# A three-layer kernel with mixtures of experts: weights placed and loaded earlier, stores moved to another queue, wide products added

## The reference, cut to what matters

```
group_idx   = top 1 of softmax(t @ router_group_w + b)          # 4 groups
exp_idx     = top 2 inside that group                           # 4 experts in each
combine     = one_hot(expert) * gate                            # [512, 16]
h = silu(t @ w_gate[e]) * (t @ w_up[e])                         # 1024 -> 256, every expert e
y = sum over e of combine[:, e] * (h @ w_down[e])               # 256 -> 1024
```

## Time and profile before

| what | value |
|---|---|
| median of 3 runs | 2019.25 us |
| profiled execution, its own time | 2021.44 us |
| its span, first to last instruction | 2019.6 us |
| PE busy | 1928.9 us (96%) |
| DVE, ACT, POOL busy | 950.5, 436.0, 326.3 us |
| mean granted TensorE clock | 0.976 |
| DMA moved | 363.86 MB, mean 180 GB/s |
| passes of the three layers, about | 849 to 1001, 1390 to 1543, 1850 to 1996 us |

### The profile page before, as it was taken

One profiled execution on the slowest core, in us unless ns is written; L12 is line 12 of the kernel. 1 busy time (PEld: TensorE's weight loads), 2 busy tenths in 40 slices (PEclk: granted clock), 3 DMA queues, 4 the chain that ended last, 5 costly groups with the idle time before them and its releaser, 6 DMA issues. The chain is left out here.

```text
span 2019.6 us, 20721 instructions
## 1 busy us (share of the span) xinstructions
PE 1928.9 (96%) x7464; PEld 1024.5 (51%) x7464; DVE 950.5 (47%) x1803; ACT 436.0 (22%) x1051; POOL 326.3 (16%) x548
## 2 busy tenths in 40 slices
PE   8999999999999999999899998999989999999995
PEld 4444444558885444544345445545434656645431
DVE  3444734547775022623363555535343367625333
ACT  1111101013333100100241105511002546612000
POOL 1000000000012000133100006502332003301333
PEclk9999999999999999999888999998998999999998
DMA  6223373730004113699834882027997102027996
GB/s 202 92 104 110 130 260 122 253 126 1 1 1 146 64 61 137 244 369 411 324 132 146 281 323 85 24 104 290 407 405 276 66 24 84 2 85 280 358 413 263
DMA packets 123017, 363.86 MB, mean 180 GB/s; under 512 B 26188, under 2 KB 31592, under 8 KB 110368
## 3 DMA queue, kind: packets, MB, share of 16 engines
q1 hardware_dynamic: 83104, 196.16, 27.2%
q10 hardware_dynamic: 25776, 133.70, 16.6%
q0 software_dynamic: 14032, 32.64, 4.5%
HBM read 335.07 MB, written 39.88 MB: 186 GB/s over the span
## 5 line engine op out<-in xcount | busy, mean ns | idle before, releaser
L1701 PE MATMUL bank<-ring,work 128*128 128x512 f32 (+1 forms) x432 | 201.5, 621 | 13.9 <-issue 13.1
L448 PE MATMUL bank<-featT,ring 128*128 128x512 f32 x384 | 168.7, 593 | 3.0 <-DMA ring<-in_w_in 3.0
L2562 PE MATMUL bank<-ring,featT 128*128 128x512 f32 x384 | 169.9, 603 | 1.6 <-DVE small L2654 1.6
L1409 PE MATMUL bank<-ring,work 128*128 128x512 f32 x384 | 166.5, 593 | 3.0 <-PEq L1200 1.1
L2059 POOL DMA_INDIRECT work<-x_rows,small x132 | 132.1, 1001 | 221.2 <-DVE work L2023 155.1
L1701 PE MATMUL bank<-work 128*128 128x512 f32 (+1 forms) x336 | 152.3, 607 | 0.0
L1701 PEld LDWEIGHTS bank<-ring,work 128*128 128x128 f32 (+1 forms) x432 | 75.9, 181 | 118.9 <-issue 118.8
L1725 DVE TENSOR_TENSOR work<-work,bank 128x256 f32<-128x256 f32 x39 | 16.4, 421 | 229.1 <-ACT work L1722 229.1
L2562 PEld LDWEIGHTS bank<-ring,featT 128*128 128x128 f32 x384 | 73.9, 194 | 93.9 <-issue 92.1
L1409 PEld LDWEIGHTS bank<-ring,work 128*128 128x128 f32 x384 | 72.2, 190 | 91.2 <-issue 91.2
L448 PEld LDWEIGHTS bank<-featT,ring 128*128 128x128 f32 x384 | 71.2, 190 | 83.9 <-issue 80.8
(11 more groups left out here) (503 smaller groups left out, 3045.9 us busy)
## 6 DMA issues: line engine op xcount, KB each, us to landing
ring<-in_w_in SPq DMA_DIRECT2D x15, 2048.0 KB, 11.7
ring_halves<-in_w_ada SPq DMA_DIRECT2D x48, 512.0 KB, 7.1
y_rows<-work ACTq DMA_DIRECT2D x39, 512.0 KB, 12.9
ring<-in_moe_w_gate ACTq DMA_DIRECT2D x14, 1024.0 KB, 9.2
ring<-in_moe_w_up ACTq DMA_DIRECT2D x14, 1024.0 KB, 12.0
ring_halves<-in_moe_w_down ACTq DMA_DIRECT2D x14, 1024.0 KB, 14.6
state<-in_w_ada SPq DMA_DIRECT2D x24, 512.0 KB, 6.5
ada_w<-in_w_ada SPq DMA_DIRECT2D x24, 512.0 KB, 7.0
```

What stands on the lines that cost most here:

```text
L448: last = nc.tensor.matmul(bank[b % 4][:, :], w[:, k, (b % 4) * P:(b % 4 + 1) * P], featT[:, k, :], start=(k == 0), stop=(k == KD - 1))
L1409: last = nc.tensor.matmul(bank[j % 4][:, :], outT[:, k, t * P:(t + 1) * P], w[:, k, :], start=(k == 0), stop=(k == KD - 1))
L1701: last = nc.tensor.matmul(gu_sum[par][at], xgT[par][:, k, at], w_gu[place_of[u]][:, k, :, :], start=(k == 0), stop=(k == KD - 1))
L2562: last = nc.tensor.matmul(f_bank(j)[:, :], featT[:, k, t * P:(t + 1) * P], w[:, k, :], start=(k == 0), stop=(k == KD - 1))
```

## The change

Five things are edited. Expert 14 moves from place 3 to place 2. `far_gu` is swapped, and of places 2 and 3 one (`ahead`: 3 in the first layer, 2 in the others) has its gate, up and down weights, and the other (`behind`) its down weights, issued by SyncE at the start of the block of the projection; the gate and up weights of `behind` are issued after the projection's last job. To make room, the first layer norm's gain and shift move from buffer 4 to buffer 2 and one block later, the normed rows of the later layers from buffer 0 to buffer 1, and two scratch tiles to buffer 2. SyncE issues the stores of all passes in a loop, and the modulation loads and the next weights take fixed turns in that loop: the first modulation loads before the store of pass 1, the last four before the store of pass 9. The biases are added in passes 11 and 12. TensorE gets three more `keep_clock(1)` before the passes.

```
         NEAR, PLACES = 2, 4
         place_of = {u: u % PLACES for u in range(NE - 2)}
-        place_of.update({NE - 2: 3, NE - 1: 0})
+        place_of.update({NE - 2: 2, NE - 1: 0})
...
-            far_gu = [buf[4], buf[0]]
+            far_gu = [buf[0], buf[4]]
+            ahead, behind = (3, 2) if gain is not None else (2, 3)
...
-            BIAS_AT = {NP - 3: (0, 1), NP - 2: (2, 3)}
+            BIAS_AT = {NP - 2: (0, 1, 2), NP - 1: (3,)}
...
                     if late:
                         late(sp)
+                    load_far_gate_up(sp, ahead, ahead)
+                    load_far_down(sp, ahead, ahead)
+                    load_far_down(sp, behind, behind)
...
-                    load_far_gate_up(sp, 2, 2)
-                    load_far_down(sp, 2, 2)
+                    PE.wait(sp, ("sum", len(jobs) - 1))
+                    load_far_gate_up(sp, behind, behind)
...
+                    def keep_clock(n):
+                        for _ in range(n):
+                            nc.tensor.matmul(bank[5][:, :], ident[:, :], level_mask[:, 0:4, :].rearrange("p a n -> p (a n)"), start=True, stop=True)
+                    keep_clock(1)
                     pass_slots()
+                    keep_clock(1)
                     turn_x(pe, 0, 0, 0)
                     parts()
+                    keep_clock(1)
                     for e in range(NP):
                         body(e)
...
-                    for par in range(2):
-                        sp.wait_ge(x_landed[par], x_due(par, 0))
-                    load_far_gate_up(sp, 3, 3)
-                    load_far_down(sp, 3, 3)
-                    if mod is not None:
-                        DV.wait(sp, ("weight", N_WEIGHT - 1))
-                        modulation_loads(sp, mod, lambda: sp.wait_ge(M_gu.sem, v(M_gu, pass_of[users[2][-1]])))
-                    W.issue(sp, 1)
+                    for e in range(NP):
+                        if mod is not None and e == 1:
+                            DV.wait(sp, ("weight", N_WEIGHT - 1))
+                            modulation_loads(sp, mod)
+                        if mod is not None and e == pass_of[users[3][-1]]:
+                            sp.wait_ge(M_gu.sem, v(M_gu, e))
+                            modulation_rest(sp, mod)
+                        if e == NP - 2:
+                            W.issue(sp, 1)
+                        for m in M_y:
+                            sp.wait_ge(m.sem, v(m, e))
+                        sp.dma_start(y_rows[bass.ds(e * P, P), :], yg[e % 2]).then_inc(y_stored[e % 2], 16)
...
                         for u in PASSES[e]:
                             if u in next_in:
                                 load_down(next_in[u])
-                        store_y(e)
```

More of the change, by code:

```diff
@@ L1184, in _ @@
             def _(sp):
-                load(sp, buf[4][:, 0:DM], D["ln1_g"].partition_broadcast(P))
-                load(sp, buf[4][:, DM:2 * DM], D["ln1_b"].partition_broadcast(P))
                 load(sp, resid[:, :, :], x_tok)
@@ L1199, in build @@
         mixed_o = [buf[3][:, i * BANK:(i + 1) * BANK] for i in range(2)]
+        ln1_g, ln1_b = buf[2][:, 0:DM], buf[2][:, DM:2 * DM]
         with nc.Block() as block:
@@ L1255, in _ @@
             def _(sp):
+                load(sp, ln1_g, D["ln1_g"].partition_broadcast(P))
+                load(sp, ln1_b, D["ln1_b"].partition_broadcast(P))
                 W.issue(sp)
@@ L1289, in build, with modulation_loads @@
         sh_cols, sc_cols, norm_cols = (small[:, 80 + KD * i:80 + KD * (i + 1)] for i in range(3))
-        def modulation_loads(sp, l, far_free):
+        def modulation_loads(sp, l):
             for i in range(4):
@@ L1300, in modulation_loads, with modulation_rest @@
                 load(sp, ada_sum[:, i * DM:(i + 1) * DM], ada_part[l, :, i * DM:(i + 1) * DM])
-            far_free()
+        def modulation_rest(sp, l):
             for i in range(4):
@@ L1344, in moe @@
             cmpx, eidf = g(144, N_EXTRA * NE), small[:, 364:364 + N_EXTRA + 1]
-            far_gu = [buf[4], buf[0]]
+            far_gu = [buf[0], buf[4]]
+            ahead, behind = (3, 2) if gain is not None else (2, 3)
+            x_back = x_tok if gain is not None else tok(buf[0])
             far_dn = [buf[2][:, 2 * DM:4 * DM], buf[6][:, 0:2 * DM] if gain is not None else buf[3][:, 0:2 * DM]]
@@ L1754, in extra_pe @@
                         for t in range(T):
-                            last = nc.tensor.matmul(bank[k // 4][:, (k % 4) * P:(k % 4 + 1) * P], eighth(x_tok[:, t, :], k),
+                            last = nc.tensor.matmul(bank[k // 4][:, (k % 4) * P:(k % 4 + 1) * P], eighth(x_back[:, t, :], k),
                                                     extra_is[:, t * P:(t + 1) * P], start=(t == 0), stop=(t == T - 1))
@@ L1780, in extra_act @@
                     if gain is None:
-                        nc.scalar.dma_start(x_tok, x_rows.rearrange("(t p) n -> p t n", p=P)).then_inc(E_in, 16)
+                        nc.scalar.dma_start(x_back, x_rows.rearrange("(t p) n -> p t n", p=P)).then_inc(E_in, 16)
                     nc.scalar.wait_ge(E_pe, 4 * x + 1)
@@ L1889, in keep_y_act @@
                         keep_y(e % 2, 0, y_bank(e, 0)).then_inc(M_y[0].sem, 1)
-                    def store_y(e):
-                        for m in M_y:
-                            act.wait_ge(m.sem, v(m, e))
-                        act.dma_start(y_rows[bass.ds(e * P, P), :], yg[e % 2]).then_inc(y_stored[e % 2], 16)
                     def keep_x_act(e):
@@ L2274, in build @@
         T4 = lambda a, n: a.rearrange("p (t n) -> p t n", t=T)
-        h_tok2 = T4(work[:, 0:T * DM], DM)
+        h_tok2 = tok(buf[1])
         DVH = DM // NHB
```

7 lines of the change are left out of this document (3 added, 4 removed).

## The result

The changed kernel takes 2037.99 us (median of 4 runs, 2036.88 to 2039.16) against 2019.14 us of the kernel before beside it (2016.26 to 2022.01): a ratio of 1.0083, 95% interval 1.0061 to 1.0105. It is slower by about 0.8%. Its profiled execution spans 2036.8 us, 17.2 more than before's 2019.6.

A forecast was written before the change was run, and what follows sets the result against it. Bound by bytes: DMA is full in the expert stages, the last load decides. Pass 12 later by 2.2, 0.7 and 6.1 us plus 4 of clock, total 13.0, gives 2032.3, stated as 2031; range 2020 to 2042, chance 0.50.

The forecast's parts named there:

- The debt and the last load: Expert stages: more bytes owed than can be moved, DMA at 1.02, so expert 15's up weights, the last load, matter.
- signs: Expert stages: shorter wait at pass 11, new one before pass 12, longest in third layer; stores landing in 5 to 8 us.
- The clock after the new wait: Pass after the wait, at the lower clock: 2 us in the third layer, 1 each in first and second.
- The composition of the landing: Expert 15's up weights, first layer: 14's down 2.6, store 1.3, gathers 1.3, modulation 2, earlier start -1; together +6.2 us.
- The gathers: GpSimd's early gathers start sooner, beside the last weights: 1.3 us in the first layer, 4.4 in the third.
- The stores: On SyncE's queue they land sooner and overtake weights; pass 9's store costs 1.3 us; no credit for the second queue.
- The first rival: Faster: pass 11's waits go and nothing is late instead; pass 12 starts at 977.7 in layer one; about 1999 us; chance 0.13.
- The second: Rival, faster by little: order and stores do not count, expert 15 lands when it did; about 2010 us; chance 0.15.
- The third: Rival, slower than forecast: gathers and modulation at full price, 2044 us and above; chance 0.08.
- The fourth: Rival: pass 11 still waits as long and pass 12 not at all; within 6 us; chance 0.14.
- The early loads and the head: Third and fourth experts' weights loaded during projection: nothing; wide products start passes 1, 2 and 0 us earlier by layer.
- The hole: DMA at 858 to 862 us, 31 GB/s, formerly filled by first modulation loads; stays empty, they cost 2 us later.

The follow-up runs named there:

- the downs after 15: Changed kernel with the down weights of experts 13 and 14 issued one pass later, behind expert 15's gate and up weights: 2014.72 us, ratio 0.9965.
- Single edits: Changed kernel with, singly: stores on ScalarE (2023.37 us); downs of 13 and 14 behind expert 15's weights (2014.72); last four sums small (2028.37); expert 14 back (2030.40).
- the first two together: Changed kernel with stores on ScalarE again and the downs of experts 13 and 14 behind expert 15's gate and up weights: 2007.22 us, ratio 0.9924.

## Why the prediction was right, and where it was not

The forecast was 2031 us with the wait moved from pass 11 to pass 12; it came to 2037.99, inside its range of 2020 to 2042. Of the 7.0 us between, the terms below lack 3.8; the forecast was rounded down by 1.3; 0.4 lie in the rest of the span, and the other 1.5 are the profiled execution, 2.2 us above its median before and 0.6 after. Taken against the routing's start, so that the layers ahead don't count, step by step:

| | layer 1 | layer 2 | layer 3 |
|---|---|---|---|
| expert 15's up weights land later: forecast | 6.2 | 5.2 | 8.3 |
| measured | 7.4 | 5.5 | 7.8 |
| pass 12 starts later: forecast | 2.2 | 0.7 | 6.1 |
| measured | 3.4 | 0.9 | 5.7 |
| pass 12 longer by the clock: forecast | 1 | 1 | 2 |
| measured | 2.6 | 2.3 | 1.9 |

(Measured start in the first layer: 990.15 - 985.14, less 1.6 by which the routing began later; the other layers likewise, less 5.3 and 9.4. The landing is the start of the load and its time, with the same taken off.) The starts sum to 10.0 for a forecast of 9.0, the clock to 6.8 for 4: 16.8 for 13.0.

**The debt and the last load: right.** That the stretch would stay full, that expert 15 would be the one to miss, that the wait at pass 11 would not hide it: all three are in the rows above. Two of its signs did not come: the new wait is not longest in the third layer but shortest (7.22 us), and the stores took longer than 5 to 8 us. One sentence of it was too strong. "The stage owes more bytes than can be moved" is not so, since the same bytes in another order take 2014.72 or 2007.22 us. They could be moved; part of what is needed later was moved sooner.

**The clock after the new wait: mis-sized.** I took only 1 us of the clock in each of the first two layers, because the wait would be divided between pass 11 and pass 12. It was divided, but not evenly: 3.02 and 2.22 us before pass 11, whose first piece kept the full clock (0.61 us), and 9.35 and 7.95 us before pass 12. The granted clock there was 0.74 and 0.76 (a mean of the levels 2.4 and 1.2 GHz), and pass 12 cost 2.6 and 2.3 us more. In these two layers the term is 2.9 us too small, out of the 3.8 that the whole sum lacks.

**The composition of the landing: partly wrong.** The landing came out nearly to size, but not from the terms that I named. The first modulation loads at 2 us measured 2.6 to 2.9. The other four sums are the missing term: my account of the change says that they go ahead of the store of pass 9, and the sum does not ask what that costs. Their issue went from 941.66 to 957.15, into expert 15's way, and is worth 4.8 us a layer by the medians (half of 9.6), 6.0 and 6.3 by the stages. The store of pass 10, 0.52 MB, also came ahead of expert 15's landing and has no term. On the other side I counted 2.6 us for 14's down and credited nothing for the stores that leave ScalarE's queue: it moved 6.50 MB for 7.06 there, no more than before. The two errors have opposite signs, so that the landing came out within 1.2 us of the forecast is in part luck.

**The gathers: right in size, wrong in what they are worth.** Third layer: 1.87 MB on GpSimd's queue before the landing, 4.5 us at 0.41 MB per us, for a forecast of 4.4. (They began 6.4 us sooner than before, counted from the routing, and not 12 as in the first layer.) But delaying them gives nothing there, since the end of the layer needs them: 4.8 us less in the stage, 7.7 more behind it. In the first two layers the stages became 2.6 and 3.2 us shorter without them, for 1.3 in the sum.

**The stores.** They land in 8.9 us (median of 39; 14.5 for the two beside expert 15), for the 5 to 8 that I wrote and 12.9 before; the 17.7 of the earlier trace rows is the store of pass 8 alone. The rule taken from the Trainium skill ("DMA: Bandwidth & Descriptors", section "Issuing engines are not separate DMA queues"), that transfers interleave on the same engines whoever starts them, agrees with the trace in the rate: 1.02 of the engines' time with one queue full or two. What that section leaves open is the order. One queue kept the stores behind the weights; two let them pass, and that is 14.6 us here, though the gathers that follow the stores are in this number.

**The first rival** fell: pass 12 has no start at 977. The advice for it in the Trainium skill ("Perfetto Trace Analysis", section "DMA Optimizations"), input and output on different engines, which the page gives as something that may make sense, made this kernel slower: with it 2037.99 us, without it 2023.37. **The second** needed a small share for the stores, with expert 15 landing when it did; SyncE's queue got 30.3% (a third of its bytes are stores) and the landing moved by 7.4 us. **The third** wanted gathers and modulation at full price, 2044 us and above; the measured time stays below that, and the modulation below its 3.8 us. **The fourth** fell with the wait at pass 11.

**The early loads and the head.** The hole stayed empty as forecast: from 840 to 862 us 63 GB/s for 207 before, 3.2 MB less, of which 1.57 are the first modulation loads and the rest weights that were loaded ahead. That the early loads delay nothing in the projection holds: no new wait shows there. That they gain nothing is not shown; undoing them cost 17 us, but in another arrangement than that of the kernel before. The head came at full clock in all three layers, with first passes 6.9 us shorter in sum. Counted from the routing the first pass ended 1.6, 3.2 and 0.0 us sooner, for the 1, 2 and 0 that I took. Without the wide products the stages are only 2.2 us longer.

Two slips of the prediction change nothing: the digits of the third stretch are 27996, and the high end of the second layer is 7.6 us by its own terms, for the 7.4 written.

## What to carry to other kernels

In a stretch in which the DMA engines are full, ask for each transfer when it is needed, and put on the same queue, behind it, whatever is needed later; a second queue for results that nobody is waiting for takes its share from the load that everybody waits for. Look for bytes that moved early at the point where the engines fall idle just after the late load has landed: they are what can be put behind it. When a place or a buffer changes hands, follow every issue that hangs on its old user, the small ones on other queues too.

## What the runs showed that I had not expected

- With three queues busy, 3.14 MB in a few large transfers on SyncE's queue took 30.3% of the engines' time beside 6.50 MB of weights on ScalarE's; the rate of all was 403 GB/s, for 421 with ScalarE's queue alone.
- A wait before a pass can cost its length and then the clock: over all kernels here pass 12 took 7.13 us behind waits of 0.95 to 1.65 us, and 8.52 to 9.91 behind waits of 2.81 to 10.34, for 7.03 to 7.13 without one. The length of the wait alone does not settle it: at pass 11 the first piece kept the full clock (0.61 us) behind 3.02 and 2.22 us in the changed kernel and 3.29 with the downs after 15, and took 1.08 behind 3.30 without the wide products. So the two downs, 2.1 MB or 5 us of transfer a layer, were worth up to 9.3 us of stage: the wait and the clock behind it went together.
- Single edits give back 14.6, 23.3, 9.6 and 7.6 us of a loss of 18.9: they relieve the same wait, and their gains can't be added; the first two together gave 30.8.
